# Shifting the on-chip layout by 64 bytes and taking out the settling matmuls in a two-block transformer kernel

## What is computed

```
for l in range(2):                                   # first block
    x = x + 0.5 * swiglu_ffn(x, ffn1...)             # 1024 -> 2816 -> 1024
    h = rms_norm(x, mix_norm[l])
    aq, ak, av, bq, bk, bv, cq, ck, cv, cg, gates = split(h @ w_in[l])
    y_a, y_b, y_c = three kinds of attention
    x = x + (sum of sigmoid(gates) * (y @ w_branch)) @ w_out[l]
    x = x + 0.5 * swiglu_ffn(x, ffn2...)
# second block: a state-space mixer with a context, then a feed-forward
x = x + gm_x * rms_norm(mixer(x, ctx)); x = x + gf_x * rms_norm(swiglu(x))
```

## Time and profile before

| | us |
|---|---|
| three runs | 1610.68, 1611.14, 1611.28 |
| median | 1611.14 |
| profiled execution, span from first to last instruction | 1610.8 |
| TensorE busy | 1596.6 |
| VectorE busy | 1288.4 |
| ScalarE busy | 927.8 |
| GpSimd busy | 212.1 |

### The profile page before, as it was taken

The page is one execution under the profiler, slowest core; times in us unless marked ns, Lnnn a source line. Parts: engine busy times, 40 slices in busy tenths (PEclk is TensorE's granted clock), DMA queues, the critical chain, the costliest instruction groups (busy, mean ns, idle before and its releaser), DMA issues.

```text
span 1610.8 us, 29874 instructions
## 1 busy us (share of the span) xinstructions
PE 1596.6 (99%) x13116; PEld 1533.9 (95%) x13116; DVE 1288.4 (80%) x1464; ACT 927.8 (58%) x1113; POOL 212.1 (13%) x125
## 2 busy tenths in 40 slices
PE   9999999999999999999999999999999999999998
PEld 8999987999999999999987899999999989899998
DVE  7887878688888888997878688785899688896655
ACT  7554656685465555554555676455556566754544
POOL 1000100000040001110010000032232367600000
PEclk9999999999999999999999999999999999999999
DMA  7677654444556665767654434555554335335551
GB/s 292 225 270 271 259 184 157 157 155 160 212 222 250 254 257 203 268 242 279 267 185 179 158 138 164 192 213 188 205 187 181 132 148 190 134 133 199 192 190 73
DMA packets 48264, 320.73 MB, mean 199 GB/s; under 512 B 5372, under 2 KB 8188, under 8 KB 10632
## 3 DMA queue, kind: packets, MB, share of 16 engines
q1 hardware_dynamic: 47992, 318.81, 53.7%
q10 hardware_dynamic: 144, 0.02, 0.0%
HBM read 317.74 MB, written 1.07 MB: 198 GB/s over the span
## 4 chain that ended last, share of the span: by engine, by line
PE 91%; DVE 5%; ACT 2%; DMA 1%; issue 0%; SPq 0%; DVEq 0%
PE ps L1240 26%; PE ps L1242 25%; PE ps L1241 25%; PE ps L1438 3%; PE ps L1440 3%; PE ps L1439 3%; DVE wlo L1907 1%; PE ps L1452 1%; ACT whi L692 1%; PE ps L1463 1%; DMA raw<-in_w_dram 1%; PE ps L1719 1%; DVE tmp L1907 1%; DVE qkA L1907 1%; DVE pre L2527 1%; PE ps L1666 0%
## 5 line engine op out<-in xcount | busy, mean ns | idle before, releaser
L1907 DVE TENSOR_TENSOR wlo<-raw,whi 128x2048 fp32r<-128x2048 f32 (+2 forms) x255 | 582.2, 2291 | 96.2 <-ACT whi L692 92.5
L692 ACT ACTIVATE whi<-raw 128x2048 fp32r<-128x2048 f32 (+1 forms) x264 | 500.0, 1906 | 211.1 <-DMA raw<-in_w_dram 210.6
L1240 PE MATMUL ps<-h1hi,whi 128*128 128x256 f32 x1792 | 500.4, 279 | 2.0 <-DVE wlo L1907 2.0
L1242 PE MATMUL ps<-h1lo,whi 128*128 128x256 f32 x1792 | 496.5, 277 | 0.0
L1241 PE MATMUL ps<-h1hi,wlo 128*128 128x256 f32 x1792 | 496.5, 277 | 0.0
L1240 PEld LDWEIGHTS ps<-h1hi,whi 128*128 128x128 f32 x1792 | 337.9, 189 | 5.5 <-issue 3.9
L1241 PEld LDWEIGHTS ps<-h1hi,wlo 128*128 128x128 f32 x1792 | 337.7, 188 | 0.1
L1242 PEld LDWEIGHTS ps<-h1lo,whi 128*128 128x128 f32 x1792 | 337.3, 188 | 0.0
L1240 PE MATMUL ps<-hid_hi,whi 128*128 128x256 f32 x880 | 243.8, 277 | 0.0
L1242 PE MATMUL ps<-hid_lo,whi 128*128 128x256 f32 x880 | 243.1, 276 | 0.0
L1241 PE MATMUL ps<-hid_hi,wlo 128*128 128x256 f32 x880 | 243.1, 276 | 0.0
(11 more groups left out here) (374 smaller groups left out, 2594.7 us busy)
## 6 DMA issues: line engine op xcount, KB each, us to landing
raw<-in_w_dram SPq DMA_DIRECT2D x288, 1024.0 KB, 4.8
from_start<-decay_dram SPq DMA_DIRECT2D x3, 768.0 KB, 4.1
raw<-in_w_dram SPq DMA_DIRECT2D x8, 256.0 KB, 5.2
c_rows<-in_c_rows_dram SPq DMA_DIRECT2D x2, 1024.0 KB, 10.2
relbias<-in_relbias_dram SPq DMA_DIRECT2D x2, 1024.0 KB, 8.4
pv<-in_pv_dram SPq DMA_DIRECT2D x2, 641.0 KB, 7.9
xT<-in_x_dram SPq DMA_DIRECT2D x4, 256.0 KB, 4.8
raw<-in_w_dram SPq DMA_DIRECT2D x2, 512.0 KB, 6.3
```

The source lines that it names most:

```text
L692: act.activation(whi[:, slot, c], raw[:, slot, c], ACT.Copy).then_inc(hi_done[slot], 1)
L1240: pe.matmul(out, w_hi, hi, start=start, stop=False, skip_group_check=skip)
L1242: return pe.matmul(out, w_hi, lo, start=False, stop=stop, skip_group_check=skip)
L1907: return dve.tensor_tensor(out, a, b, op)
```

## The change

The start of the layout goes from 1280 to 1344, and `operand_base` pads to 0 instead of 192 modulo 256. Every tile so moves up by 64 bytes: the slots of the ring begin at 64 and the activation tiles at 0 modulo 256. The function `settle`, the constant `SETTLED` and all calls of it are gone.

```diff
-SETTLED = (3, 7)
...
-    base = [1280]
+    base = [1344]
...
     def operand_base():
 
-        base[0] += (192 - base[0]) % 256
+        base[0] += -base[0] % 256
         return base[0]
...
-    assert ring0 % 256 == 0
+    assert ring0 % 256 == 64
...
     for first in (hhi0, g0, a0, c0, t0, base[0]):
-        assert first % 256 == 192, first
+        assert first % 256 == 0, first
...
-        def settle(bank):
-
-
-            cols = ones[:, :].rearrange("p (m s n) -> p m s n", m=2, s=2)
-            for q in range(4):
-                ins = pe.matmul(ps[32 * q:32 * q + 32, bank, 256:320].rearrange("p (m n) -> p m n", m=2), ones[:, 0:32],
-                                cols[:, :, q % 2, :], start=True, stop=True, tile_position=(0, 32 * q))
-            return ins
...
-            def chunk(g, bank, settled=False):
+            def chunk(g, bank):
...
-                if settled:
-                    settle(bank)
...
                     if j == 0:
                         strips(bank, slot, (ctxT,))
-                        settle(bank)
...
-                    settle(bank).then_inc(cdt_done, 1)
+                    ins.then_inc(cdt_done, 1)
...
-                    if i == 6:
-                        settle(7 - 2 * (i % 2))
...
-            settle(6)
...
-                chunk(g0 + 3 * i - 1, 4 + 2 * (i % 2), f < 3 and i in SETTLED)
+                chunk(g0 + 3 * i - 1, 4 + 2 * (i % 2))
...
-            gate_slab(3, True)
+            gate_slab(3)
...
-                if q == 3:
-                    settle(0)
```

More of the change, by code:

```diff
@@ L260, in build_program @@
     v0 = base[0]
-    assert v0 % 256 == 192
+    assert v0 % 256 == 0
     h1hi = sb("h1hi", [P, KT, S], F32R)
@@ L1477, in gate_half, with gate_slab @@
                     ins.then_inc(used[slot], 1)
-            def gate_slab(k, settled=False):
+            def gate_slab(k):
                 bank = (k + 2) % 4
```

## The result

The changed kernel takes 1616.41 us (median of 20 runs, 1608.55 to 1624.26); the kernel before, over as many runs, 1611.51 (1608.92 to 1615.56). The ratio is 1.0038, 95% interval 1.0027 to 1.005 (the two medians alone give 1.0030): slower by 0.3 to 0.4%, and no longer steady. All ratios here leave out runs in a slow state, of which the record has three: one at 1981 us in each of the two kernels at the distances 160 and 224, with a granted clock of 0.75, and one at 5708 us of the kernel before. The 20 times stand in three heaps: three from 1608.6 to 1610.2, eight from 1615.0 to 1616.5, nine from 1620.3 to 1624.3. One feed-forward of 1,488 `block3` matmuls at 117.8 ns instead of 113.3 is 6.6 us (4.45 ns each), about the distance between two heaps.

What follows compares the result with a forecast made beforehand. The prediction took TensorE's issue rate as the bound (busy 99%). From a span of 1610.8 us, -8.3 for groups and -4.8 for slow matmuls gave 1597.7; plus 0.3, 1598.0 us. The 8-in-10 range was 1588 to 1632.

Steps and rivals of the forecast that it cites:

- The groups' own cost, -8.3 us: In TensorE's own chain, removing 18 settling groups at 0.46 us each saves 8.3 us.
- I take 113.3 without the slow alternative: After the shift every `block3` matmul runs at 113.3 ns; the 1,074 slow ones gain 4.45 ns each, -4.8 us.
- The sentence on the even shift: Both operands move 64 bytes, so their distance stays 192 modulo 256 and unsettled `block3` stretches stay a coin's toss.
- first rival: In `block3` the slow cadence stays and nothing settles it: 5,784 slow matmuls, +25.7 less 8.3, 1628.5 us; chance 0.28.
- what follows sums is slow: In the first three feed-forwards, 1,488 matmuls behind the opening sums were counted as running at 117.8 ns.
- The projections at 0: The 864 projection matmuls keep 228.9 ns, a term of 0, with ends from -13.5 to +5.8 us.
- TensorE's waits still under 10 us: A sign that the forecast is right: TensorE's waits in the changed profile stay under 10 us.
- DVE at 80% has room: VectorE, which makes the low halves of weights, was taken to have room for a faster TensorE.
- its cover for late weights: TensorE's 2.0 us of weight waits were taken to hide longer transfers: 0, with +-0.5 us for the first slab.
- The 0.3 us between span and time: Execution time was taken as 0.3 us above the span, making 1597.7 into 1598.0.
- The rule against it: By the skill's separate read ports, tile start addresses cannot set TensorE's cadence, which would make the first rival right.
- the 109.2 ns that the prediction set beside this: The page's N/2.4 + 2.5 cadence for 256-column `block3` matmuls: 45 us more saved, to 1553; chance 0.03.

Runs made afterwards that it cites:

- the first profile: The changed kernel (64-byte shift, no settling groups) against the kernel before, profiled with its 20-run measurement: 1616.41 us, ratio 1.0038.
- the two profiles: The changed kernel, without further edits, profiled in two measurements against the kernel before: 1616.41 us (ratio 1.0038) and 1621.86 us (ratio 1.0053).

## Why the prediction was wrong

The forecast was 1598.0 us; it came out at 1616.41, within the stated range but on the other side of no change. Step by step:

- **The groups' own cost, -8.3 us: right.** 0.46 us each from the earlier trace rows, 0.5 from the lowest run of the kernel without six of them.
- **"I take 113.3 without the slow alternative", -4.8 us: the step that failed.** In its place the first profile has 2,965 more matmuls at 117.8: +13.2 us where the sum had -4.8, so what the groups keep away was priced at nothing. The term rested on the earlier trace rows: the projections' moving tile begins at 0, and they had one cadence. Both halves were wrong. For `block3` what counts is the distance between the operands, 64 there and 192 in `block3`, and not the place of one of them; and the projections have a second cadence, 233.3, which that profile did not show. The shift keeps every distance, and alone it left the time where it was (0.9992). The sentence on the even shift in the first rival was the right reading, and I gave it 0.28 against 0.52.
- **The first rival, 1628.5 us: right in its mechanism, too high by its count.** It counted 5,784 newly slow matmuls; the two profiles have 4,039 and 5,240 matmuls at 117.8 ns in all, 2,965 and 4,166 more than before. The term that was mis-sized is the 4,464 matmuls of the first three feed-forwards. I read the earlier trace rows as "what follows sums is slow". They are two cases of turning over from fast: where the slow branches came first, the sums ended the slow cadence, and the second feed-forward was fast in both profiles. And a pause before a slab can turn it over again, a place that I had not counted at all, since the profile of before shows no such pause inside the first three feed-forwards. Pauses of 0.15, 0.16, 0.16 and 0.24 us turned fast to slow, others of 0.14, 0.25 and 0.36 did not.
- **The projections at 0: nearly right.** +1.0 us in the profile, inside the stated ends. Where the feed-forward ahead of them ends slow they are slow too, in this layout.
- **"TensorE's waits still under 10 us": right, but they were not harmless.** The busy times of DVE and ACT moved by 1 us. Yet the pause that made the third feed-forward slow is a wait for VectorE's low halves: 0.24 us of it, and 1,344 x 4.45 ns = 6.0 us behind it. The prediction's "DVE at 80% has room" and its cover for late weights priced the wait alone.
- **The 0.3 us between span and time: too small.** Every later record has both, and the time is 1.7 to 2.0 us above the span (1615.94 and 1614.0, for one). By this the execution profiled before took about 1612.7 us, above the three times printed beside it. With this the forecast would have been 1599.6, which changes nothing else. The row of the granted clock shows tenths, in which the stretch at 0.50 is lost.
- **The rule against it.** The Trainium skill, "TensorE: Matmul & The Clock Gate", section "Step-by-step: what each phase is for", gives each operand a read port of its own; by that, the cadence would not depend on where tiles begin. For the shift of this change that came nearly true, for another reason: the kernel at the distance 0 is 3.0% slower than the one at 192 without groups (1666.48 and 1618.31 us), and their edits differ in the padding alone. Where in the chip the two reads would meet is not shown. No run came near the 109.2 ns that the prediction set beside this; the fastest cadence is 113.3.

What remains open: why the pairs are 113.3 and 117.8, 228.9 and 233.3, and which property of an interruption decides, since pauses and groups of the same length had both outcomes. The table of distances was measured with one pair of places each but for 0 and 192. Why the groups of the first feed-forward failed in two kernels was not tried.

## What to carry to other kernels

Where a stream of equal matmuls bounds a kernel, read the distance from start to start stretch by stretch: 4.5 ns in 113 is invisible in the busy share and was worth 13 us here. Before trusting that one operand's address matters, move both and move one; and before calling a repair idle at a place, ask what state it finds there in the kernel in which it is to be removed. A repair that is paid on the critical path is worth the chance of need times the chance that it works times what it saves, so it belongs ahead of long stretches and behind what is known to disturb them. And before taking work away from a busy engine, look where it arrives next: 0.5 us earlier was enough to meet a late operand.

## What the runs showed of the hardware

- The cadence of a 128-column weight load with a 256-column float32r matmul depends on the distance of the two operands in SBUF, given here modulo 256 bytes: 120.0 ns at 0, 117.8 (seldom 113.3) at 64, 118.7 at 128, 117.3 or 118.7 at 160, 113.3 or 117.8 at 192, 118.3 at 224. With 512 columns the order is another: from 226.7 at 0, 228.9 or 233.3 at 64 (the projections of the kernels with 192 for `block3`), 233.3 at 192.
- At the distance 192 two cadences are stable. The slow one held for 1,344 to 1,536 matmuls, where the profile of before had 192 at most. A pause of 0.07 to 0.24 us ended the fast one in five places inside a feed-forward; pauses of 0.14 to 0.36 us left it alone in three.
- A single float32 matmul of 256 columns between two stretches turned the cadence over in 20 of 20 token sums and in 7 of 7 of the context's, always within the distance 192; the same sum in two halves of 128 kept it in all eight cases, the context's sum included.
- A group of four float32 matmuls of 32 by 64 between two stretches at the distance 192 left a fast cadence fast 28 times in 28 and ended a slow one 10 times in 16.
